# Expert weights in 4 MB transfers with 32 KB runs, in a hybrid attention and mixture-of-experts block

## What is computed

```python
def moe_ffn(h, router_w, router_b, w_gate_up, b_gate_up, w_down, b_down):
    logits = (hf @ router_w).astype(jnp.float32) + router_b.astype(jnp.float32)
    top_v, top_e = lax.top_k(logits, TOP_K)
    top_w = jax.nn.softmax(top_v, axis=-1)
    ...
    def expert_block(args):
        xb, e = args
        gu = xb @ w_gate_up[e] + b_gate_up[e]
        gate = jnp.minimum(gu[:, 0::2], SWIGLU_LIMIT)
        up = jnp.clip(gu[:, 1::2], -SWIGLU_LIMIT, SWIGLU_LIMIT)
        glu = gate * jax.nn.sigmoid(gate * SWIGLU_ALPHA)
        return ((up + 1.0) * glu) @ w_down[e] + b_down[e]
```

## Time and profile before

| | us |
|---|---|
| median of 3 runs | 1136.11 (1135.65 to 1136.47) |
| the profiled execution's own time | 1136.25 |
| its span, first to last instruction | 1134.5 |
| TensorE busy in the span | 1059.2 (93%) |
| TensorE's weight loads | 519.9 (46%) |
| VectorE busy | 348.4 (31%) |
| ScalarE busy | 222.7 (20%) |
| GpSimd busy | 38.9 (3%) |
| DMA | 439.17 MB in 47489 packets, 387 GB/s over the span |

### The profile page before, as it was taken

One profiled execution on the slowest core, in us unless ns is written; L12 is line 12 of the kernel. 1 busy time (PEld: TensorE's weight loads), 2 busy tenths in 40 slices (PEclk: granted clock), 3 DMA queues, 4 the chain that ended last, 5 costly groups with the idle time before them and its releaser, 6 DMA issues.

```text
span 1134.5 us, 13360 instructions
## 1 busy us (share of the span) xinstructions
PE 1059.2 (93%) x5613; PEld 519.9 (46%) x5613; DVE 348.4 (31%) x686; ACT 222.7 (20%) x354; POOL 38.9 (3%) x32
## 2 busy tenths in 40 slices
PE   7999999999999999999988888888888898899896
PEld 7889999734343443434333333333333334233332
DVE  4984788422303222222222222222112020303022
ACT  6645674201010101011010010101010101010002
POOL 0390000000000000000000000000000000000000
PEclk9999999999999999999999999999999999999999
DMA  9545669999999999999999999999999999999994
GB/s 320 190 150 215 231 215 365 368 415 415 430 428 428 426 430 427 428 428 427 429 426 428 427 428 428 428 429 426 429 428 428 428 426 428 428 427 427 428 425 201
DMA packets 47489, 439.17 MB, mean 387 GB/s; under 512 B 5388, under 2 KB 7848, under 8 KB 22600
## 3 DMA queue, kind: packets, MB, share of 16 engines
q1 hardware_dynamic: 45136, 436.71, 92.6%
q10 hardware_dynamic: 2296, 1.61, 0.5%
HBM read 437.26 MB, written 1.05 MB: 386 GB/s over the span
## 4 chain that ended last, share of the span: by engine, by line
PE 57%; DMA 41%; DVE 1%; issue 0%; ACT 0%; another core or an unknown queue 0%; DVEq 0%
DMA S<-in_w_gate_up_dram 21%; PE PS L1671 20%; DMA S<-in_w_down_dram 12%; PE PS L1730 9%; PE PS L1338 9%; DMA B<-in_w_gate_up_dram 4%; PE PS L1652 4%; DMA EXTRA<-in_w_gate_up_dram 4%; PE PS L1632 3%; PE PS L1351 1%; PE PS L1354 1%; PE PS L1357 1%; PE PS L1712 1%; PE PS L1692 1%; PE PS L1318 1%; PE PS L1389 1%
## 5 line engine op out<-in xcount | busy, mean ns | idle before, releaser
L1671 PE MATMUL PS<-S,M 128*64 128x512 f32 x1520 | 340.0, 596 | 28.5 <-DMA S<-in_w_gate_up_dram 22.0
L1671 PEld LDWEIGHTS PS<-S,M 128*64 128x64 f32 x1520 | 105.3, 137 | 241.9 <-issue 195.7
L1171 DVE TENSOR_SCALAR M<-PS 128x256 f32<-128x256 f32 x64 | 27.0, 423 | 531.8 <-PE PS L1671 531.8
L1730 PE MATMUL PS<-S,M 128*64 128x512 f32 x736 | 164.7, 595 | 17.1 <-DMA S<-in_w_down_dram 17.1
L765 ACT ACTIVATE M<-M 128x256 f32<-128x256 f32 x64 | 26.7, 417 | 495.4 <-DVE M L1171 495.4
L1730 PEld LDWEIGHTS PS<-S,M 128*64 128x64 f32 x736 | 52.0, 137 | 119.8 <-issue 102.5
L770 ACT COPY M<-PS 64x512 f32<-64x512 f32 x31 | 17.9, 578 | 276.4 <-PE PS L1730 276.4
L1185 DVE COPY M<-PS 128x512 f32<-128x512 f32 x32 | 22.1, 692 | 127.7 <-PE PS L1712 127.7
L1632 PE MATMUL PS<-M,X 128*128 128x128 f32 x480 | 59.0, 281 | 0.0
L1632 PEld LDWEIGHTS PS<-M,X 128*128 128x128 f32 x480 | 57.7, 196 | 0.0
L1652 PE MATMUL PS<-M,SELT 128*128 128x512 f32 x120 | 55.5, 605 | 0.0
(11 more groups left out here) (259 smaller groups left out, 978.3 us busy)
## 6 DMA issues: line engine op xcount, KB each, us to landing
S<-in_w_gate_up_dram SPq DMA_DIRECT2D x95, 2048.0 KB, 47.8
S<-in_w_down_dram SPq DMA_DIRECT2D x43, 2048.0 KB, 47.2
M<-in_w_gate_up_dram SPq DMA_DIRECT2D x12, 2048.0 KB, 46.5
EXTRA<-in_w_gate_up_dram SPq DMA_DIRECT2D x11, 2048.0 KB, 48.7
S<-in_w_in_dram SPq DMA_DIRECT2D x10, 2048.0 KB, 7.9
B<-in_w_gate_up_dram SPq DMA_DIRECT2D x10, 2048.0 KB, 48.5
B<-in_w_down_dram SPq DMA_DIRECT2D x7, 2048.0 KB, 48.2
EXTRA<-in_w_down_dram SPq DMA_DIRECT2D x6, 2048.0 KB, 48.0
```

What stands on the lines that cost most here:

```text
L1171: v.tensor_scalar(gate[:, c], g2[:, :, 0], LIMIT, None, ALU.min).then_inc(gate_ready, 1)
L1671: ins = mm(gu[half][64 * g:64 * g + 64, :], hTe[:, k, tok], gu_slot[slot][:, kk, c:c + 512], start=(k == 0), stop=(k == KD - 1))
L1730: ins = mm(dst[64 * n:64 * n + 64, :], actT[b][:, k, 64 * kh:64 * kh + 64], dn_slot[slot][:, k, 512 * n:512 * n + 512], start=(kh == 0 and ...
```

## The change

Loads m and m + 1 (m even) become one transfer of 4 MB, in which a partition has four gate rows or eight down rows, one run of 32 KB. The ring of eleven slots stays, but all its slots now lie side by side in one tensor W (M shrinks to eight pages, EXTRA is gone), so that two neighbours can be filled by one DMA; positions 9 and 10 of the ring (the two ends of W) are not adjacent. `by_slots` says which pairs of slots are still loaded singly: those whose first slot has ring position 9, all of pair 0, the first four loads of pair 1 and the last eight of the last pair. A single load has runs of 16 KB at a distance of 32 KB. `load_unit` waits until both slots are used. Semaphores count by m and no longer by slot. `arrived` waits for a whole unit at its even m.

As four gate rows lie in a partition, `hidden` reads every fourth column, `n2w` follows. The gate product's halves are also cut another way: half 0 and 1 are the lower and upper 1024 columns, and the two products of a half take alternate pieces of eight columns (`cols[:, :, g, :]`). The biases are laid out to match: two groups of four DMAs in place of one, the second issued after `squares(1, 1)`; four copies in place of one and four subtractions in place of one, each 512 columns for 64 and 32 partitions.

```diff
-        wgu = A["w_gate_up"].rearrange("l e (s p k) n -> (l e) s p (k n)", p=P, k=2)
-        wdn = A["w_down"].rearrange("l e (h p c) n -> (l e) h p (c n)", p=P, c=4)
+        wgu = A["w_gate_up"].rearrange("l e (u p k) n -> (l e) u p (k n)", p=P, k=4)
+        wdn = A["w_down"].rearrange("l e (p c) n -> (l e) p (c n)", p=P)
...
+        def slots(n, count=1):
+
+            at = (n + 1) % SLOTS
+            return W[:, 4096 * at:4096 * (at + count)]
...
+        def by_slots(j, m, first_round):
+
+            return not first_round or ring(j, m) == 9 or j == 0 or j == 1 and m < 4 or j == PAIRS - 1 and m >= 4
...
+            def load_unit(e, j, m):
+
+                sp.dma_start(slots(ring(j, m), 2), unit_src(e, m)).then_inc(slot_loaded[m], 16)
...
+            def load_pair(p, e, j, first_round, stop=12):
+
+                for m in range(0, stop, 2):
+                    if by_slots(j, m, first_round):
+                        for n in (m, m + 1):
+                            used(p + (n - SLOTS) // 12, (n - SLOTS) % 12)
+                            load(e, j, n)
+                    else:
+                        for n in (m, m + 1):
+                            used(p + (n - SLOTS) // 12, (n - SLOTS) % 12)
+                        load_unit(e, j, m)
...
+            for x in range(4):
+                se.dma_start(bias_raw[1][E * x:E * x + E, :], b_gu[1]).then_inc(bias_loaded, 16)
             filled(se, "lg1")
-            se.wait_ge(bias_loaded, 64)
-            st.did(nc.scalar.copy(bias_parts, bias_raw), bias_hi_ready)
+            se.wait_ge(bias_loaded, 128)
+            for g in range(2):
+                for half in range(2):
+                    to, raw = bias_cols(g, half)
+                    st.did(nc.scalar.copy(to[64 * g:64 * g + 64], raw[64 * g:64 * g + 64]), bias_hi_ready)
...
             def hidden(tt, k):
-                return X[:, tt, 256 * (k // 2) + k % 2:256 * (k // 2) + 256:2]
+                return X[:, tt, 512 * (k // 4) + k % 4:512 * (k // 4) + 512:4]
...
                 def one(half, k, slot, kk):
+                    cols = gu_slot[slot][:, kk, 1024 * half:1024 * half + 1024].rearrange("p (j g r) -> p j g r", g=2, r=8)
                     for g in range(2):
-                        c = 1024 * g + 512 * half
-                        ins = mm(gu[half][64 * g:64 * g + 64, :], hTe[:, k, tok], gu_slot[slot][:, kk, c:c + 512],
-                                 start=(k == 0), stop=(k == KD - 1))
+                        ins = mm(gate_rows(half, g), hTe[:, k, tok], cols[:, :, g, :], start=(k == 0), stop=(k == KD - 1))
```

More of the change, by code:

```diff
@@ L334, in hybrid_block @@
         half_used, half_loaded = sem("half_used"), sem("half_loaded")
[L335 removed]
+        slot_loaded = [sem(f"slot_loaded{m}") for m in range(12)]
         part_loaded = [sem(f"part_loaded{n}") for n in range(3)]
@@ L403, in load @@
             def load(e, j, m):
-                slot = ring(j, m)[0]
-                sp.dma_start(slots[slot], slot_src(e, m)).then_inc(slot_loaded[slot], 16)
+                sp.dma_start(slots(ring(j, m)), slot_src(e, m)).then_inc(slot_loaded[m], 16)
+            def load_unit(e, j, m):
+                sp.dma_start(slots(ring(j, m), 2), unit_src(e, m)).then_inc(slot_loaded[m], 16)
             for n, what in enumerate(LOADS):
                 if what == GB1:
-                    load(0, 0, 9)
+                    load(0, 0, 8)
                 if what == "mu":
@@ L454, in used @@
                     sp.wait_ge(weights_used, p * 8 + (m - m // 4 if m < 8 else 6 + (m - 8) // 2) + 1)
[L456 to L463, removed]
+            def load_pair(p, e, j, first_round, stop=12):
[8 more added lines that the diff above has]
+                        load_unit(e, j, m)
+            for part, done in ((0, half_loaded), (1, slot_loaded[11])):
                 if part == 0:
@@ L479, in _ @@
                     used(last + (m - SLOTS) // 12, (m - SLOTS) % 12)
-                sp.dma_start(slots[ring(last, m)[0]][:, 1024 * c0:1024 * c1],
-                             wdn[E - 1, m - 10, :, 1024 * c0:1024 * c1]).then_inc(done, 16)
+                sp.dma_start(slots(ring(last, m))[:, 1024 * c0:1024 * c1],
+                             slot_src(E - 2, m)[:, 1024 * c0:1024 * c1]).then_inc(done, 16)
             sp.wait_ge(rounds_ready, 1)
@@ L1205, in _ @@
             bias_selector(0)
-            ve.wait_ge(bias_hi_ready, 1)
-            st.did(v.tensor_tensor(bias_parts[2 * E:4 * E], bias_raw[2 * E:4 * E], bias_parts[2 * E:4 * E], ALU.subtract),
-                   bias_ready)
+            ve.wait_ge(bias_hi_ready, 4)
+            for g in range(2):
+                for half in range(2):
+                    to, raw = bias_cols(g, half)
+                    rest = slice(64 * g + 32, 64 * g + 64)
+                    st.did(v.tensor_tensor(to[rest], raw[rest], to[rest], ALU.subtract), bias_ready)
             ve.wait_ge(lgexp_ready, TT)
@@ L1658, in arrived, with gate_rows @@
                 r, j = at
-                slot, before = ring(j, m)
-                pe.wait_ge(slot_loaded[slot], r * (16 * PER_ROUND[slot]) + (before * 16 + 16))
-                return slot
+                slot = ring(j, m)
+                if m % 2 == 0:
+                    pe.wait_ge(slot_loaded[m], r * (16 * PAIRS) + 16 * (j + 1))
+                elif isinstance(r, int):
+                    if by_slots(j, m - 1, True):
+                        pe.wait_ge(slot_loaded[m], 16 * odd_loads(m, True, j + 1))
+                else:
+                    pe.wait_ge(slot_loaded[m], r * (16 * PAIRS) + 16 * (odd_loads(m, True) - PAIRS + j + 1))
+                return slot
+            def gate_rows(half, g):
+                return gu[half][64 * g:64 * g + 64, :].rearrange("p (j r) -> p j r", r=8)
             def gate_up(at, i, m, b, opening, between=None):
```

84 lines of the change are left out of this document (45 added, 39 removed).

## The result

The changed kernel takes 1140.44 us in the median of six runs (1138.49 to 1140.96), the kernel before 1135.88 in six runs beside it (1134.45 to 1137.32). The ratio is 1.004 [1.003, 1.005]: slower by 4.6 us. The profiled execution has a time of 1140.96 and a span of 1138.9 us, at a granted clock of 0.997.

A forecast was written before the change was run, and what follows sets the result against it. The weight stream plus a fixed tail was taken as the bound. Longer runs -5.7, a later stream +3.6 (1.2 + 2.4) and the tail +1.6 gave -0.5 us: 1135.6 us from 1136.11, range 1131.5 to 1141.5.

The forecast's parts named there:

- What bounds the kernel: Whole kernel: the weight stream at 428 GB/s sets the end, plus a fixed tail; TensorE comes 12% behind it.
- Longer runs, -5.7 us: Weight stream: 76 double loads each save 8 runs an engine at 9.3 ns, 5.7 us in all; bounds 0 and 8.0.
- Rival A: Weight stream: a run's own cost is smaller, at the end nothing; without any saving 1141.3 us; chance 0.16.
- The opening: Start of the expert part: a later TensorE delays the stream; stride-of-four weight loads were taken at 0.3 us a gather.
- In the later pairs TensorE's 7.0 us cover it: Later expert pairs: TensorE's spare 7.0 us per pair against the stream hides the slower gather, so nothing was charged.
- Rival C: Gather: weight loads at a stride of 16 bytes are slow, 3.9 us at the opening; +1.0, 1137.1 us; chance 0.10.
- s = 2.4: Opening: biases complete at 233.6, the bias product before at 231.22, so TensorE starts 2.4 us later; bounds 0 and 5.
- The hold, +1.2 net: Early pair 1: double loads wait for both slots while only two loads are in flight; net loss 1.2 us.
- The tail, +1.6: Last pair: joined loads start m = 3 later, waits absorb part; last product 1.6 us later against the stream; bounds 0 and 2.
- Pieces of eight, nothing: Gate product: its moving operand, read in pieces of eight floats, was taken to cost nothing, 3.6 us a slot unchanged.
- rival D: Gate product: pieces of eight slow it; at twice the time some 350 us more for the kernel; chance 0.04.

## Why the prediction was wrong

I had forecast 1135.6 us and no change that can be told; it is 1140.44, slower, near the upper end of the range. By its steps:

**What bounds the kernel: right.** In the middle the stream is the bound and got faster; what is lost is lost where its queue is short.

**Longer runs, -5.7 us: right.** 9.3 ns a run was taken from two rates; 8.6 to 8.9 was measured in three pairs of kernels, 5.2 us for the 76 loads. The steady rate is 430 for the 431 of the forecast. Rival A is false. The Trainium skill's figure of 3 cycles a packet ("DMA: Bandwidth & Descriptors", section "Why small descriptors are slow"), 1.8 us by my estimate for 65 loads, is under the 4.45 us measured for them: the two rates of the trace were the better guide.

**The opening: the failed step, in the sentence on the stride of four.** I took 0.3 us a gather, "since doubling the stride once has cost 7 ns". It is 3.7 us (7.63 against 3.93): one doubling says nothing of the next. The trace of before could not show that, but it was the term with the widest bounds, 0 to 3.93, and I took it near the lower one. The Trainium skill's rule ("SBUF — State Buffer", section "Specifications (TRN2)": two hits on a line of 16 bytes) agrees with the measured curve: 197 ns at two floats, 318 to 330 at four.

**"In the later pairs TensorE's 7.0 us cover it": failed too.** This is true from pair 1 on: in the kernel before with a stride of four the stream goes at 427 and 429 GB/s from 300 to 320 and from 320 to 340 us. But pair 0 has a gather of its own, at 269 us, with two or three loads in flight. There a later TensorE goes to the stream. Rival C had the mechanism, with a chance of 0.10, and the same gap: it counted one 3.9 in place of s = 2.4 and so came to +1.0 only. The stride alone, in the kernel before, cost 5.7. "One for one" was a little too much: TensorE was 7.4 us late behind pair 0's gather there, and 5.7 came out at the end.

**The biases, s = 2.4: right as a time, wrong in its effect.** They are ready at 234.4; 233.6 was forecast, and the front part is 0.9 later. In the changed kernel TensorE comes later than they do, so they cost nothing. Where it does come in time, the wait of 2.67 us costs 4.3, the fallen clock included; the clock was in none of my cases.

**The hold, +1.2 net: mis-sized.** 3.3 us in the kernel with fast gathers; in the changed one 4.0 us with the saving of the nine long loads taken off, so some 4.6 by itself. The first gap was right, 2.1 us for 2.0. For the second held load, issued 2.5 us before the first was to have landed, I had 0.2 us; it cost 1.2. And I took off what the kernel before loses by itself (369 GB/s from 274 to 280, some 0.8 us), which the kernel with X reordered mostly doesn't (412).

**The tail, +1.6: right in kind.** 1.0 us in the profiled executions, and no wait at m = 7 to 11, as forecast. The run that took the last pair's double loads away didn't get it back in time, so the 1.0 rests on the timelines alone. In the kernel with X reordered the same joining costs 3.8 us by the timelines, as TensorE waits 3.56 us and its clock falls.

**Pieces of eight, nothing: right.** 3.65 us a slot as before; rival D is false.

With the measured terms the sum is -5.2 + 5.7 + 3.3 + 1.0 = +4.8 us, against 4.6 measured. The terms come from different kernels and need not simply add (the slow gather and the hold meet in the same short queue), so this is a check of size, not more. In the changed kernel alone the steps are 5.6 us (all loads single), -4.7 (67 double loads), +4.0 (nine more in pairs 1 and 2), 4.9 in all. The bytes fit too: by them the stream is 1.06 slots or 5.2 us behind at 1000 us, and 0.96 slot or 4.7 us at 1080, as it goes on catching up. The landing in the last pair is only 3.6 us later because at that moment 0.2 slot less of the loads behind it is in, another 1.0 us.

## What to carry to other kernels

Longer runs pay by a fixed time per run and can be priced from two rates with full engines; but where a layout change for the DMAs changes the stride of a stationary operand, price that stride by a measurement, or reorder the data once when it is written. Delay on a compute engine costs what the queue of loads doesn't cover: near the start, with two or three loads in flight, most of it goes to the end (5.7 of 7.4 us, 4.3 of 5.7), and there transfers should also go out singly and be joined only once the queue is deep. A wait of TensorE can cost more than its length, as the clock can fall behind it (2.67 us of wait, 4.3 us of time); check for it wherever a wait is moved or uncovered.

## What the hardware showed that was not expected

A weight load of 128 x 128 float32 takes some 191, 197, 256, 330 ns at strides of 1, 2, 3, 4 floats, and stays between 318 and 336 up to 8. The loads and their matmuls overlap: a gather of 32 takes 3.93 us at a stride of two and 7.63 at four.

After idle times of 2.67 us (biases) and 3.56 us (last pair) the granted clock stood at 1.2 GHz for 6.8 us each (233.9 to 240.7, and from 1080.0), and after the second a product of 16 instructions took 6.50 us in place of 3.65. The length of the idle time alone doesn't settle it: after 2.04 us in the last pair the product took 3.65 in the kernel before, and 5.35 in the kernel with X reordered and all loads single. Products that compute nothing, put into such a wait, kept the clock at 1.00. A fallen clock costs only where TensorE is waited for: in the middle of the kernel with X reordered the granted clock is 0.98 in the mean, and the stream still goes at 430 GB/s.

Runs of 16 KB at a distance of 32 KB in SBUF go as fast as contiguous ones: 428 GB/s in both.
